# A new order of issue in the second mixing stage: exponentials, quotients, weight splits, and the turn of the merged rows

## What is computed

```python
hn = rms_norm(h, mix_norm_g)
z = hn @ w_in                       # latents, pool input, gate_a, gate_b
q_lat, kv_lat, k_rope, u_pool, gate_a, gate_b = split(z)
q  = rms_norm(q_lat)  @ w_q_up      # 8 heads of 64 + 32 (rotated)
kv = rms_norm(kv_lat) @ w_kv_up
attn = softmax(mask(q k / sqrt(96))) v     # 8 heads, block-causal
y_a = attn @ w_attn_branch
y_b = multiscale_pool(u_pool) @ w_pool_branch
h = h + (sigmoid(gate_a) * y_a + sigmoid(gate_b) * y_b) @ w_mix_out
h = h + memory_cross_attention(...)
h = h + hierarchical_moe(...)       # 32 experts, 2 chosen
return rms_norm(h, final_norm_g)
```

## Time and profile before

| | us |
|---|---|
| median of 3 runs | 1026.51 (1026.29 to 1026.66) |
| the profiled execution, its own time | 1027.73 |
| its span, first to last instruction | 1025.9 |
| PE busy in it | 980.0 |
| DVE, ACT busy | 541.8, 476.3 |

### The profile page before, as it was taken

How to read it: one execution, slowest core, us unless ns; L and a number is a source line. 1 busy time by engine, 2 the same in 40 slices (tenths; PEclk the granted TensorE clock), 3 DMA queues, 4 the chain that set the end, 5 groups by cost and what they waited for, 6 DMA issues and landing times.

```text
span 1025.9 us, 13609 instructions
## 1 busy us (share of the span) xinstructions
PE 980.0 (96%) x5479; PEld 744.6 (73%) x5479; DVE 541.8 (53%) x868; ACT 476.3 (46%) x761; POOL 0.8 (0%) x8
## 2 busy tenths in 40 slices
PE   9999998998999999999999988998999999999995
PEld 8779786876889888998899866788774454454442
DVE  5788795665566556545766852755462122122114
ACT  5488555555345544443766562354342232222222
POOL 0000000000000000000000000000000000000000
PEclk9999999999999999999999999999999999999998
DMA  9744466323455445654446533465197999999991
GB/s 296 253 164 167 162 206 204 121 86 124 164 185 195 175 164 172 232 182 155 148 136 217 196 115 121 145 229 167 47 323 260 395 391 395 394 392 395 391 397 54
DMA packets 107268, 223.53 MB, mean 218 GB/s; under 512 B 10185, under 2 KB 15042, under 8 KB 107202
## 3 DMA queue, kind: packets, MB, share of 16 engines
q1 hardware_dynamic: 104752, 219.10, 60.4%
q10 hardware_dynamic: 2450, 3.51, 1.2%
HBM read 221.54 MB, written 1.05 MB: 217 GB/s over the span
## 4 chain that ended last, share of the span: by engine, by line
PE 80%; DVE 9%; ACT 5%; issue 3%; SPq 2%; DMA 1%; ACTq 0%; DVEq 0%
PE pb L461 17%; PE pb L463 16%; PE pb L462 16%; PE pb L2311 11%; PE pb L2334 5%; PE pb L2286 3%; PE pb L2349 3%; DVE wl L1460 2%; ACT wh L937 2%; PE pb L524 1%; DMA raw<-in_w_in 1%; SPq L429 1%; PE pb L595 1%; PE pb L664 1%; PE pb L2260 1%
## 5 line engine op out<-in xcount | busy, mean ns | idle before, releaser
L1460 DVE TENSOR_TENSOR wl<-raw,wh 128x2048 fp32r<-128x2048 f32 (+2 forms) x113 | 248.8, 2209 | 141.8 <-ACT wh L937 141.6
L937 ACT ACTIVATE wh<-raw 128x2048 fp32r<-128x2048 f32 (+2 forms) x114 | 208.4, 1836 | 132.1 <-PE pb L463 123.3
L461 PE MATMUL pb<-wh,th 128*128 128x512 f32 (+2 forms) x620 | 249.7, 403 | 3.5 <-DVE tl L1515 2.4
L462 PE MATMUL pb<-wl,th 128*128 128x512 f32 (+2 forms) x620 | 243.4, 393 | 0.0
L463 PE MATMUL pb<-wh,tl 128*128 128x512 f32 (+2 forms) x620 | 243.2, 392 | 0.0
L461 PE MATMUL pb<-th,wh 128*128 128x256 f32 x544 | 155.7, 286 | 1.3 <-DVE wl L1460 1.1
L463 PE MATMUL pb<-th,wl 128*128 128x256 f32 x544 | 153.5, 282 | 0.0
L462 PE MATMUL pb<-tl,wh 128*128 128x256 f32 x544 | 153.2, 282 | 0.0
L461 PEld LDWEIGHTS pb<-wh,th 128*128 128x128 f32 x620 | 118.0, 190 | 31.6 <-issue 6.1
L463 PEld LDWEIGHTS pb<-wh,tl 128*128 128x128 f32 x620 | 118.0, 190 | 26.1
L462 PEld LDWEIGHTS pb<-wl,th 128*128 128x128 f32 x620 | 118.2, 191 | 23.3
(11 more groups left out here) (359 smaller groups left out, 1090.7 us busy)
## 6 DMA issues: line engine op xcount, KB each, us to landing
raw<-in_w_in SPq DMA_DIRECT2D x31, 1024.0 KB, 5.0
raw<-in_w_up SPq DMA_DIRECT2D x16, 1024.0 KB, 5.7
raw<-in_w_down SPq DMA_DIRECT2D x16, 1024.0 KB, 4.8
raw<-in_w_exp_gate SPq DMA_DIRECT2D x20, 512.0 KB, 9.6
raw<-in_w_exp_up SPq DMA_DIRECT2D x20, 512.0 KB, 11.4
raw<-in_w_exp_down SPq DMA_DIRECT2D x10, 1024.0 KB, 13.9
raw<-in_w_xkv SPq DMA_DIRECT2D x8, 1024.0 KB, 5.1
mwh<-in_w_exp_gate SPq DMA_DIRECT2D x14, 512.0 KB, 10.6
```

The costliest lines, as they stand in the source:

```text
L461: PE.matmul(o, lh, rh, start=start, stop=False, skip_group_check=True)
L462: PE.matmul(o, lh, rl, start=False, stop=False, skip_group_check=True)
L937: ACTE.activation(hi_of(i), raw_of(i), ACT.Copy).then_inc(S["hi"], 1)
L1460: DVE.tensor_tensor(lo_of(i), raw_of(i), hi_of(i).bitcast(F), ALU.subtract).then_inc(S["lo"], 1)
```

## The change

Only the order of issue changes.

PE: the row of factors is asked for one place later, and the turns of q follow by one; in the gates' units values and turns move forward, and those of group 5 that stood in the pool branch move into the last gates unit; the first four turns of merged rows move from behind the attention branch into its second unit. ACT: high halves of two latent units go ahead of the copies of the latents; exponentials and values go ahead of gates and high halves. DVE: a latent unit's split goes ahead of the norm's factor; the maxima of group 5 go ahead of a split, its quotients ahead of two; the turn of the first merged half goes ahead of the second half's sum. The last two waits named `free` are set to match.

```diff
-            pe_features(("lat", 2), 0, 2, 0, None, {1: row_mix2, 3: lambda: turn_q(0), 4: lambda: turn_q(1), 6: lambda: turn_q(2)})
+            pe_features(("lat", 2), 0, 2, 0, None, {2: row_mix2, 4: lambda: turn_q(0), 5: lambda: turn_q(1), 7: lambda: turn_q(2)})
...
                         (2, 1): {3: lambda: (PE.wait_ge(S["pool_lo"], 4), pe_turn_probs(4, 0, 24)),
-                                 7: lambda: (pe_values(4, 0), pe_turn_probs(4, 1))},
-                        (3, 0): {3: lambda: pe_values(4, 1)},
-                        (3, 1): {5: lambda: pe_turn_probs(5, 0)}}
+                                 5: lambda: (pe_values(4, 0), pe_turn_probs(4, 1))},
+                        (3, 0): {1: lambda: pe_values(4, 1), 5: lambda: pe_turn_probs(5, 0)},
+                        (3, 1): {1: lambda: (pe_values(5, 0), pe_turn_probs(5, 1)), 5: lambda: pe_values(5, 1)}}
...
-            pe_tokens(("w_pool_branch_2", 0), 0, 1, 1, 0, 512, lambda kk: (S["pool_lo"], kk + 1),
-                      {1: lambda: (pe_values(5, 0), pe_turn_probs(5, 1)), 5: lambda: pe_values(5, 1)})
+            pe_tokens(("w_pool_branch_2", 0), 0, 1, 1, 0, 512, lambda kk: (S["pool_lo"], kk + 1))
...
-            for b in range(2):
-                pe_tokens(("w_attn_branch_2", b), 0, 1, 1, 4, 512, (lambda kk: (S["o_lo"], 8 + kk - 3)) if b == 0 else None)
...
-            turn_m2(range(4))
+            pe_tokens(("w_attn_branch_2", 0), 0, 1, 1, 4, 512, lambda kk: (S["o_lo"], 8 + kk - 3))
+            pe_tokens(("w_attn_branch_2", 1), 0, 1, 1, 4, 512, None, {5: lambda: turn_m2(range(4))})
... ACT
             act_unit("lat", 1, 0)
             act_unit("lat", 0, 1)
+            act_unit("lat", 1, 1)
+            act_unit("lat", 2, 0)
             act_done(("lat", 0), 1)
             ACTE.wait_ge(*scaled("mix2"))
...
             act_probs(4, 0)
             act_exps(5, 0)
-            act_gates("gates2", 2, (S["pooled"], 8))
-            act_unit("gates2", 3, 0)
             act_values(4, 0, (S["used"], U["w_kv_up_2", 1, 0] + 1))
             act_probs(4, 1)
             act_exps(5, 1)
+            act_unit("gates2", 3, 0)
+            act_values(4, 1)
+            act_gates("gates2", 2, (S["pooled"], 8))
+            act_probs(5, 0)
             act_unit("gates2", 3, 1)
-            act_values(4, 1)
-            act_probs(5, 0)
-            act_gates("gates2", 3)
-            act_unit("w_pool_branch_2", 0, 0)
             act_values(5, 0)
             act_probs(5, 1)
+            act_values(5, 1)
+            act_unit("w_pool_branch_2", 0, 0)
+            act_gates("gates2", 3)
             act_unit("w_pool_branch_2", 1, 0)
-            act_values(5, 1)
... DVE
+            dve_unit("lat", 0, 1)
             dve_scale("mix2", ssq["ple"], D, rs_of["mix2"], ...)
-            dve_unit("lat", 0, 1)
...
             dve_masked(5, 1)
+            dve_max(5)
             dve_unit("gates2", 2, 0)
             dve_probs(4)
             dve_unit("gates2", 2, 1)
-            dve_max(5)
+            dve_values(4, 0)
+            dve_probs(5)
+            dve_values(4, 1)
             dve_unit("gates2", 3, 0)
-            dve_values(4, 0)
+            dve_values(5, 0)
             dve_unit("gates2", 3, 1)
-            dve_values(4, 1)
-            dve_probs(5)
-            dve_unit("w_pool_branch_2", 0, 0)
-            dve_values(5, 0)
-            dve_gated("w_pool_branch_2", 0, 0, GB)
-            dve_unit("w_pool_branch_2", 1, 0)
             dve_values(5, 1)
-            dve_gated("w_pool_branch_2", 0, 1, GB)
-            for b in range(2):
-                dve_unit("w_attn_branch_2", b, 0)
-                dve_gated("w_attn_branch_2", 0, b, GA, into=GB)
+            for b in range(2):
+                dve_unit("w_pool_branch_2", b, 0)
+                dve_gated("w_pool_branch_2", 0, b, GB)
+            dve_unit("w_attn_branch_2", 0, 0)
+            dve_gated("w_attn_branch_2", 0, 0, GA, into=GB)
             dve_turn("m2", range(4), None, 1, scale=0.5)
+            dve_gated("w_attn_branch_2", 0, 1, GA, into=GB)
+            dve_unit("w_attn_branch_2", 1, 0)
             for b in range(2):
                 for r in range(2):
-                    dve_unit("w_mix_out_2", b, r)
                     if (b, r) == (0, 0):
                         dve_turn("m2", range(4, 8), None, 1, scale=0.5)
+                    dve_unit("w_mix_out_2", b, r)
```

More of the change, by code:

```diff
@@ L1315, in act_main @@
                                 scale=rs_of["mix2"][:, t:t + 1]).then_inc(evicted(("lat", 0))[0], 1)
-            act_unit("lat", 1, 1)
             act_done(("lat", 1), 1)
@@ L1320, in act_main @@
                                 scale=rs_of["mix2"][:, t:t + 1]).then_inc(evicted(("lat", 1))[0], 1)
-            act_unit("lat", 2, 0)
             ACTE.wait_ge(S["row_mm"], 2)
@@ L1379, in act_main @@
             act_exps(5, 1)
+            act_unit("gates2", 3, 0)
+            act_values(4, 1)
+            act_gates("gates2", 2, (S["pooled"], 8))
+            act_probs(5, 0)
             act_unit("gates2", 3, 1)
-            act_values(4, 1)
-            act_probs(5, 0)
-            act_gates("gates2", 3)
-            act_unit("w_pool_branch_2", 0, 0)
             act_values(5, 0)
             act_probs(5, 1)
+            act_values(5, 1)
+            act_unit("w_pool_branch_2", 0, 0)
+            act_gates("gates2", 3)
             act_unit("w_pool_branch_2", 1, 0)
-            act_values(5, 1)
             for b in range(2):
                 act_unit("w_attn_branch_2", b, 0)
-            act_turn("m2", range(4), None, 1, scale=0.5, free=[(S["used"], U["w_attn_branch_2", 1, 0] + 1)])
+            act_turn("m2", range(4), None, 1, scale=0.5, free=[(S["used"], U["w_pool_branch_2", 1, 0] + 1)])
             for b in range(2):
@@ L1395, in act_main @@
                     if (b, r) == (0, 0):
-                        act_turn("m2", range(4, 8), None, 1, scale=0.5)
+                        act_turn("m2", range(4, 8), None, 1, scale=0.5, free=[(S["used"], U["w_attn_branch_2", 1, 0] + 1)])
                     if (b, r) == (1, 0):
```

## The result

| | before | after |
|---|---|---|
| median, us | 1026.59 (1026.29 to 1026.92, 4 runs) | 1016.75 (1014.66 to 1017.78, 4 runs) |
| ratio | | 0.9901, 95% interval 0.9884 to 0.9919 |
| profiled execution, own time | 1027.73 | 1016.10 |
| its span | 1025.9 | 1014.3 |

The change makes the kernel 9.8 us faster by the medians. The forecast was a gain of 15.1 us, the number 1011.4 and a range up to 1017.5: the direction and the range held, the number was 5.3 us too good.

The account below looks back on a forecast made before the run. PE (TensorE) bounds the kernel; its waits, with clock and overlap, were worth 15.8 us. Waits and overlap 10.4, clock 3.9 and step 1's 0.8 sum to 15.1, so 1011.4 us from the median; range 1009.8 to 1017.5.

Parts of the forecast that it names:

- steps 2 to 5: Values, quotients and merged rows: PE's waits and their overlap go, 10.4 us, plus 3.9 us of clock.
- step 1: Latent units: splitting unit 84 before the norm's factor ends PE's 1.1 us wait; 0.4 to 0.5 at row_mm; net gain 0.8.
- a new wait: Rival: late gates' copies or merged sum leave one 2 to 3 us wait plus clock loss; about 1015.5 us; chance 0.12.
- steps 4 and 5: Group 5 values in the last gates unit, and merged rows: waits of 0.54 and 2.4 us go, margins 0.3 to 2.4.
- steps 2 to 4: Fourth head group's values, group 5's quotients, group 5's values: PE's waits of 3.8, 3.2 and 0.54 us go.
- step 5: Merged rows, turned inside the second attention unit: the 2.4 us wait goes; a 0.1 us wait at the second four turns.
- Step 2: Fourth head group's first values: 3.8 us wait goes, margin 2.6; group 5's maxima cost nothing in DVE's 2.28 us gap.
- The two stretches counted as won: Low clock after the 3.8 us values wait (2.4 us lost) and the 2.4 us mix_out wait (1.5): 3.9 us won.
- the clock rival: Low stretches come elsewhere: one behind the wait at 714, 1012.9 us; the whole 3.9 us stays, 1015.3; chance 0.12.
- The shift of the expert stage: After mix_out everything is released by counters PE moves on, so it shifts as one, PE still fully busy.
- no change: Rival: the expert stage is bound by its weight loads and waits 15 us in all; 1026.5 us; chance 0.05.
- slower: Rival: weights do not follow, PE waits at expert pairs with low clock; 1031.4 us; chance 0.03.

Follow-up runs that it names:

- experiments 1 and 2: Changed kernel with the latent part (PE, ACT, DVE) put back, 1013.91 us; kernel before with the latent part alone, 1030.84 us.
- experiment 5: lat_undone with the turn of the merged rows also put back behind the attention branch (the run turn_undone): 1016.14 us.
- experiment 10: lat_undone with ACT's gates of unit 95 and high half of unit 98 put back ahead of the first values' copy: 1018.52 us.
- experiments 10 and 11: lat_undone with one place at the values put back, on ACT (gates and high half first), 1018.52 us, or on DVE (split of unit 98 first), 1019.49 us.
- experiment 6: lat_undone with the maxima of group 5 put back behind the split of unit 97 (the run max_late): 1012.8 us.
- lat_dve_old: Changed kernel with only DVE's order at the latents put back (factor first, then split of unit 84): 1017.09 us.
- lat_act_old: Changed kernel with only ACT's order at the latents put back (copies of first latent block before two high halves): 1017.45 us.
- early_high: lat_undone with the high half of unit 83 moved ahead of the norm's four squares on ACT: 1013.53 us, run again 1013.37 us.
- experiments 8 to 11: On one chip: lat_undone again, 1014.5 us; early_high again, 1013.37; lat_undone with ACT's order at the values put back, 1018.52, or DVE's, 1019.49.
- lat_undone: Changed kernel with the latent part (PE, ACT and DVE) put back as before: 1013.91 us; run again on another chip, 1014.5 us.
- lat_only: Kernel before with the latent part of the change alone: 1030.84 us, ratio 1.0045.
- turn_undone: lat_undone with the turn of the merged rows also put back behind the attention branch (PE, ACT and DVE): 1016.14 us.
- max_late: lat_undone with the maxima of group 5 put back behind the split of unit 97: 1012.8 us, ratio 0.9861.

## Why the prediction was right, and where it was too good

The waits of steps 2 to 5 went as forecast, and so did their clock. The missing 5.3 us are step 1, which came out 4.0 us worse than forecast, and a low stretch at the third scores, 1.45 us; together 5.5. The measured gain of 9.8 us lies outside the 13.5 to 16 called the forecast. It fell into the stated range because the range made room for a new wait and for the clock, but the new wait was looked for in steps 4 and 5, and came in step 1, where none was expected. So the range held in part by luck.

- **Step 1 failed, and it is most of the error.** It said: "ACT's copies of the latents come after two more high halves, but start at 537.2, when the factor is there, and end by 538.4; PE asks for them a place's 12 matmuls after the row, at 539.0." PE asks for them earlier. pe_features begins unit 84 with a wait for freed(("lat", 2)), the banks of every second block in GROUPS; these are the PSUM banks of ("lat", 0), which the copies empty. The step's own times would have given it: copies done at 538.4, unit 84 wanted at 535.4, a wait of 3.0 us against the 2.9 measured. Before, the factor came first and the copies were done when the split of unit 84 was. With the split ahead of the factor, the factor ends 1.6 us after unit 83 does, and the copies 1.05 later. In place of a gain of 0.8 us the wait grew from 1.1 to 2.9 us and drew a low stretch: 3.2 us lost in the timelines, 2.8 and 4.4 by the medians of experiments 1 and 2. The forecast's gain less 4.0 is 11.1 us. The 0.4 to 0.5 us forecast at the row of factors (L530) did not come, since the factor was long there when PE, held by the banks, reached it at 539.17.
- **Steps 2 to 5 held together.** Their sum with the clock, 10.4 + 3.9 = 14.3 us, is what the two timelines give between the rotated q and the cross attention: 13.07 + 1.25 = 14.3. The two parts hold each by itself: steps 2 to 4 with the first low stretch were 10.3 us in the sum and are 114.34 - 104.00 = 10.3 with the turn undone, and step 5 with its low stretch was 4.0 and is 3.95 (experiment 5). The first values' low half ended at 607.9 and PE's matmul that waits for it started at 610.5 with no wait, a margin of 2.7 us (2.6 forecast; the two lines stand at experiment 10). What stood in ACT's and DVE's queues was in fact what held PE (experiments 10 and 11).
- **Step 2, the remark on the gap, was wrong:** "without that gap they would push the quotients, and PE with them, by 2 us". They push the quotients, and PE does not notice (experiment 6, where they come 2.2 us later). A delay is paid only past the margin, and I had the margins in the same text.
- **Step 5** held to the tenth: the second four turns start 0.2 us late (a wait of 0.1 was expected), and undone, the wait of 2.4 us is back with a low stretch (experiment 5).
- **The clock.** The two stretches counted as won did go: the granted clock is 1.00 from 540 to 700 us. It was forecast as 1.00 from 535 on, and the new wait broke that. But the wait at 714, kept, drew one when it came at 704: 1.45 us back, the smaller of the two sizes that the clock rival gave. Waits of the same 2.75 us at the same scores (2.7 to 2.8 in all) went with a low stretch in the profiles of after, lat_dve_old, lat_act_old, early_high and the four kernels of experiments 8 to 11, and not in those of before, lat_undone, lat_only, turn_undone and max_late. The kernel of lat_undone has it in one of its two profiles. The Trainium skill ("TensorE: Matmul & The Clock Gate", Part 1) says that the gate's transitions do not start afresh with the kernel and vary from run to run; the second half is what these profiles show, the first no run here tests.
- **The shift of the expert stage** held: the lead is 11.64 us at its start and 11.6 at the end, and in all thirteen profiles the time from the first gather to the last matmul is 246.0 us. The rivals "no change" and "slower", which had their price there, found nothing.

lat_undone and early_high beat both the kernel before and the changed one; early_high is the better of the two, 1013.4 and 1013.5 us in its two experiments. (max_late, run once, took 1012.8, and no difference between its order and lat_undone's was found.)

## What to carry to other kernels

When an engine's next block of work is costed, list every wait at its head, the one for its output banks too, and follow each to the queue that raises it; in a scheme where blocks alternate between two pairs of banks, the evacuation of the last block but one is always on that list. When a wait has two queues behind it, moving work in one of them shows nothing or harm: mend both, and test each alone to learn that both were needed. And compare a delay with the margin that it falls into before giving it a price. Where the clock blurs the medians, compare the time between two equal instructions in both profiles, stage by stage.

## What was not expected of the hardware

The runs of one kernel differ by as much as 5 us, half of what this change wins and more than most edits of the experiments: the kernel before took 1026.29 to 1026.92 us in the runs first seen and 1024.59 to 1029.6 in the later ones. Most of this goes with low stretches of the clock: the mean granted clock of these runs was 0.987 to 0.992, lowest in the longest run, and 0.001 of it is about 1 us here. A wait of TensorE of 2.35 to 4.1 us cost its length and often more: a low stretch over or behind it took a further 1.4 to 1.8 us in most cases, 2.4 at the old wait for the first values and 3.0 in lat_undone_b, and nothing where the clock stayed (the 3.2 us before the quotients in the earlier trace rows, and five of the thirteen waits at the third scores). Nothing that was read from the traces tells beforehand which.
